# Convolutional feed-forward: seven half-block products for eight in the down projections of the full turns, with the sums kept tokens-on-partitions

## What is computed

```python
def conv_ffn(h, w_up, conv_w, conv_b, w_down):
    seq = h.shape[1]
    u = h @ w_up
    up = jnp.pad(u, ((0, 0), (CONV_W - 1, 0), (0, 0)))
    u = sum(up[:, j:j + seq] * conv_w[j] for j in range(CONV_W)) + conv_b
    a, b = u[..., :D_FF_2], u[..., D_FF_2:]
    return (jax.nn.silu(a) * b) @ w_down

x = x + conv_ffn(rms_norm_2(x, norm_ffn_g[i]), f_w_up[i], f_conv_w[i], f_conv_b[i], f_w_down[i])
```

## Time and profile before

| what | value |
|---|---|
| median of 3 runs | 2540.43 us (2539.84 to 2540.81) |
| the profiled execution | 2541.5 us |
| its span, first to last instruction | 2539.7 us |
| PE busy | 2495.9 us, 98% |
| POOL busy | 1654.6 us, 65% |
| DVE busy | 1280.0 us, 50% |
| ACT busy | 795.7 us, 31% |
| granted TensorE clock | 0.998 of full speed |

### The profile page before, as it was taken

One profiled execution on the slowest core, in us unless ns is written; L12 is line 12 of the kernel. 1 busy time (PEld: TensorE's weight loads), 2 busy tenths in 40 slices (PEclk: granted clock), 3 DMA queues, 4 the chain that ended last, 5 costly groups with the idle time before them and its releaser, 6 DMA issues.

```text
span 2539.7 us, 34091 instructions
## 1 busy us (share of the span) xinstructions
PE 2495.9 (98%) x12467; PEld 2033.0 (80%) x12467; DVE 1280.0 (50%) x2205; ACT 795.7 (31%) x1405; POOL 1654.6 (65%) x2010
## 2 busy tenths in 40 slices
PE   8999999999999999999989999999999999999999
PEld 6778788887787878888667888888888887888887
DVE  7444765427666567533785443435343243543432
ACT  3443432215545434322554211113112113311111
POOL 5355677866664666686652777777665755877774
PEclk9999999999999999999999999999999999999999
DMA  5122555532221366452320333232322321433231
GB/s 145 43 78 83 133 139 143 133 100 79 71 82 51 101 132 151 131 133 75 100 68 25 93 100 100 91 105 87 100 74 76 99 68 65 117 100 100 89 110 67
DMA packets 281536, 243.50 MB, mean 96 GB/s; under 512 B 14291, under 2 KB 247740, under 8 KB 281276
## 3 DMA queue, kind: packets, MB, share of 16 engines
q1 hardware_dynamic: 267692, 216.11, 27.9%
q0 software_dynamic: 13056, 25.17, 5.9%
q10 hardware_dynamic: 656, 0.43, 0.1%
HBM read 239.59 MB, written 2.10 MB: 95 GB/s over the span
## 4 chain that ended last, share of the span: by engine, by line
PE 80%; DVE 11%; issue 3%; POOL 2%; ACT 2%; DVEq 1%; DMA 1%; ACTq 0%; POOLq 0%
PE proj L753 21%; PE proj L755 21%; PE proj L754 21%; POOL w_lo L1916 2%; PE proj L2993 1%; PE proj L2994 1%; PE proj L2992 1%; DVE s_lo L1426 1%; DVE top L2508 1%; DVEq L2511 1%; PE aux L1301 1%; PE aux L1302 1%; PE aux L1303 1%; PE proj L1301 1%; PE aux L3006 1%
## 5 line engine op out<-in xcount | busy, mean ns | idle before, releaser
L753 PE MATMUL proj<-a_hi,w_hi 128*128 128x512 f32 x1864 | 739.2, 397 | 0.1
L755 PE MATMUL proj<-a_hi,w_lo 128*128 128x512 f32 x1864 | 726.5, 390 | 0.0
L754 PE MATMUL proj<-a_lo,w_hi 128*128 128x512 f32 x1864 | 726.0, 389 | 0.0
L1964 POOL TENSOR_TENSOR pool_carrier<-small 128x1 f32<-128x1 f32 x393 | 92.7, 236 | 660.6 <-PE proj L755 545.7
L1987 POOL TENSOR_TENSOR w_lo<-raw,w_hi 128x512 fp32r<-128x512 f32 (+2 forms) x393 | 517.6, 1317 | 5.3
L1986 POOL TENSOR_TENSOR w_lo<-raw,w_hi 128x512 fp32r<-128x512 f32 x330 | 430.6, 1305 | 27.5
L753 PEld LDWEIGHTS proj<-a_hi,w_hi 128*128 128x128 f32 x1864 | 350.2, 188 | 81.3 <-issue 9.1
L755 PEld LDWEIGHTS proj<-a_hi,w_lo 128*128 128x128 f32 x1864 | 350.2, 188 | 74.0
L754 PEld LDWEIGHTS proj<-a_lo,w_hi 128*128 128x128 f32 x1864 | 350.4, 188 | 73.6 <-issue 2.9
L753 PE MATMUL proj<-g_hi,w_hi 128*128 128x512 f32 x720 | 283.5, 394 | 2.5 <-DVE g_lo L740 2.3
L755 PE MATMUL proj<-g_hi,w_lo 128*128 128x512 f32 x720 | 280.4, 389 | 0.0
(11 more groups left out here) (430 smaller groups left out, 3810.7 us busy)
## 6 DMA issues: line engine op xcount, KB each, us to landing
raw<-in_mlp_w SPq DMA_DIRECT2D x52, 1024.0 KB, 5.5
raw<-in_f_w_up SPq DMA_DIRECT2D x88, 512.0 KB, 4.9
raw<-in_b_w_in SPq DMA_DIRECT2D x24, 1024.0 KB, 5.2
F<-in_mlp_w POOLq DMA_DIRECT2D x36, 512.0 KB, 5.7
raw<-in_f_w_down SPq DMA_DIRECT2D x18, 1024.0 KB, 5.2
raw<-in_hgrn_w_in SPq DMA_DIRECT2D x32, 512.0 KB, 4.9
raw<-in_b_w_out SPq DMA_DIRECT2D x8, 1024.0 KB, 5.0
F<-in_mlp_w SPq DMA_DIRECT2D x6, 1024.0 KB, 7.9
```

The costliest lines, as they stand in the source:

```text
L753: pe.matmul(psum[r][:], w_hi[r][:, w], xh, start=k == 0 and not begun, stop=False, skip_group_check=begun)
L754: pe.matmul(psum[r][:], w_hi[r][:, w], xl, start=False, stop=False, skip_group_check=begun)
L755: last = pe.matmul(psum[r][:], w_lo[r][:, w], xh, start=False, stop=k == kc - 1, skip_group_check=begun)
L1964: pool.tensor_tensor(pool_carrier[:], zero, zero, ALU.add)
```

## The change

Both full turns of both layers become seven stages. `ffn_stages` builds two `SevenStage`s of 8 pair slabs and two quarter slabs, and one stage for the last 6 blocks. `SevenStage` takes the number of its up units from its slabs (16 here, 8 in the MLP). The methods for sums, weights and products move from `Mlp` into a common class `Sevens`, and `Ffn` derives from it. `Ffn` keeps its four first products in F, its sums s1 and s4 share a PSUM bank with the silu side, and s2 lies in SBUF (`log_ms`). The products are added into `acc`. In the first layer the last stage turns these sums by 32 transposes into its banks; in the second layer DVE adds the last stage's banks into `acc`, where ACT and DVE copied before. The retention tables share space with the sums and are loaded later. The main part of the diff:

```diff
+            sevens = [seven_stage(pairs(t * DC, DC), down, t) for t in range(FULL)]
...
             def pe(self, pe):
...
+                    for j in range(0 if t else 2, st.ups):
+                        unit(pe, st, j, DC, a_hi, a_lo)
+                    self.seven_pe(pe, st, t)
...
+                pe.wait_ge(*taken_sums(self.sevens[-1], 7))
+                unit_pair(pe, st, 2 * size, size, g_hi, g_lo, 0, self.split.low.at,
+                          lambda u: self.turn_sums(pe, psum[st.bank(u)], u - 2 * size, BOTH))
...
             def act(self, act, h_at):
...
+                    act.activation(u, self.x[s][j % 2], ACT.Identity, bias=conv_col(self.l, 3, c),
+                                   scale=conv_col(self.l, 2, c)).then_inc(tap2.sem, 1)
+                    if st.SEVEN and j >= DC - 2:
+                        self.high_weights(act, st, j - (DC - 2), s)
+                    if s == 0:
+                        act.wait_ge(*tap0.at(2 * j))
+                        act.activation(self.x[0][j % 2], u, ACT.Silu).then_inc(silu.sem, 1)
+                for t, st in enumerate(self.sevens):
+                    for j in range(DC):
+                        first = j < KS
+                        gate(st, self.taps[t], j, 0, t * DC + j)
+                        if 1 <= j <= KS:
+                            self.high_first_sum(act, t, j - 1)
+                        elif j > KS:
+                            self.high_second_sums(act, t, j - 1 - KS)
+                        gate(st, self.taps[t], j, 1, t * DC + j + FF2C)
+                        act.wait_ge(*self.whole.at(j, t))
+                        there, src = (self.LEFT, self.kept[j]) if first else (slice(0, T), self.raw_at[j % 2])
+                        act.copy(tile(g_hi, j)[:, there], src[:, there]).then_inc(self.x_high.sem, 1)
+                    self.high_second_sums(act, t, KS - 1)
+                    for p in range(2, st.PRODUCTS):
+                        for h in range(2):
+                            self.high_weights(act, st, p, h)
...
             def dve(self, dve, then=None):
...
+                    for j in range(DC):
+                        if j >= KS + 2:
+                            dve.wait_ge(*self.low_at("s4", j - 2 - KS, t))
+                        project(st, j, 0)
+                        if 1 <= j <= KS:
+                            self.first_rows(dve, t, j - 1)
+                        elif j > KS:
+                            self.second_rows(dve, t, j - 1 - KS)
+                        if j == DC - 1:
+                            self.low_weights(dve, st, 0)
+                        mix(st, taps, j, 0, t * DC + j)
+                        project(st, j, 1)
+                        if 1 <= j <= KS:
+                            self.first_sum(dve, t, j - 1)
+                        elif j > KS:
+                            self.second_sums(dve, t, j - 1 - KS)
+                        if j == DC - 1:
+                            self.low_weights(dve, st, 1)
+                        mix(st, taps, j, 1, t * DC + j + FF2C)
+                        product(taps, j, self.kept[j] if j < KS else self.raw_at[j % 2]).then_inc(self.whole.sem, 1)
+                    self.second_rows(dve, t, KS - 1)
+                    self.second_sums(dve, t, KS - 1)
+                    self.take_products(dve, st, t)
...
+                if self.l == 1:
+                    for n in range(2):
+                        for b in range(TB):
+                            bank = self.out_arrived(dve, st, size, n, b)
+                            sums = acc[:, bass.ds(b * D + n * T, T)]
+                            dve.tensor_tensor(sums, bank[:], sums, ALU.add).then_inc(dve_out.sem, 1)
+                    return
...
-                        if st is st_dsa_o and q == 0:
+                        if st is ffn[0].st and q == 4:
+                            sp.wait_ge(unit_done, st.before.done(st.before.at(6, 1)))
                             ret_tables()
```

More of the change, by code:

```diff
@@ L415, in program, with seven_stage, quarter @@
         SEVENS = FF // D - 1
+        def seven_stage(ups, down, t):
+            def quarter(k, n):
+                return down[:, t * DC + k * KS:t * DC + (k + 1) * KS, n * T:(n + 1) * T]
+            quarters = [Slab(KS, units, lambda i, n=n: [(0, T, quarter(1, n))], across=True) for n, units in ((0, 14), (1, 0))]
+            stages.append(SevenStage(stages[-1], ups + quarters, sum(st.SEVEN for st in stages), t, quarter))
+            return stages[-1]
         def mlp_stages(l):
@@ L421, in ups @@
                 return [plain(mlp_w1[l], col=lambda i, c=c: t * D + c * 256) for c in range(4)]
[L423 to L430, removed]
+            sevens = [seven_stage(ups(t), down, t) for t in range(SEVENS)]
             return sevens, stage(1, ups(SEVENS) + [plain(mlp_w2[l], k0=SEVENS * DC, col=lambda i, c=c: c * 256) for c in range(4)])
@@ L1639, in down_by_token @@
             def down_by_token(self, pe, st, size, split):
-                before, _, size_before, *_ = self.parts[0]
-                for c in range(DC):
-                    emptied(pe, before, 2 * size_before + c, before.turns - 1)
                 for n in range(2):
@@ new lines, in pe @@
+                for t, st in enumerate(self.sevens):
+                    if t == 0:
+                        unit(pe, st, 0, DC, a_hi, a_lo, ready=self.pre.low.at)
+                        unit(pe, st, 1, DC, a_hi, a_lo)
+                        self.pre.norm.sum(pe)
+                    for j in range(0 if t else 2, st.ups):
+                        unit(pe, st, j, DC, a_hi, a_lo)
+                    self.seven_pe(pe, st, t)
+                st, size = self.st, self.size
+                for j in range(2 * size):
+                    unit(pe, st, j, DC, a_hi, a_lo)
@@ L1726, in dve @@
+                st, first, size, split = self.st, self.first, self.size, self.split
+                for j in range(size):
+                    for s in range(2):
+                        gate(st, self.taps[FULL], j, s, first + j + s * FF2C)
+                    act.wait_ge(*split.whole.at(j))
+                    act.copy(tile(g_hi, j), self.x[1][j % 2]).then_inc(split.high.sem, 1)
             def dve(self, dve, then=None):
                 dve.wait_ge(*self.pre.norm.ready())
-                l = self.l
@@ new lines, in dve, with rest @@
+                st, first, size, split, taps = self.st, self.first, self.size, self.split, self.taps[FULL]
+                dve.wait_ge(*taken_sums(self.sevens[-1], 7))
+                def rest(j):
+                    dve.wait_ge(*split.high.at(j))
+                    dve.tensor_tensor(tile(g_lo, j), self.x[1][j % 2], tile(g_hi, j).bitcast(F32),
+                                      ALU.subtract).then_inc(split.low.sem, 1)
+                for j in range(size):
+                    for s in range(2):
+                        project(st, j, s)
+                        if s == 0 and j >= 1:
+                            rest(j - 1)
+                        mix(st, taps, j, s, first + j + s * FF2C)
+                    product(taps, j, self.x[1][j % 2]).then_inc(split.whole.sem, 1)
@@ L1770, in program @@
+                then.dve_paced(dve, DC - 1)
         ffn = [Ffn(0)]
```

469 lines of the change are left out of this document (230 added, 239 removed).

## The result

| | before | after |
|---|---|---|
| median | 2541.51 us (2539.66 to 2545.21) | 2547.55 us (2544.92 to 2550.72) |
| the profiled execution, its span | 2541.5, 2539.7 us | 2544.92, 2543.1 us |
| ratio, with its 95% interval | | 1.0022 [1.0015, 1.003] |

The change makes the kernel slower by 0.2%: 6 us between the medians, 3.4 us between the two profiled executions (the one of after is the quickest of its runs). The forecast was 2541.6 us with a range of 2536 to 2558: the median is inside the range and 6.0 us above the forecast.

A forecast was written before the change was run, and what follows sets the result against it. PE was taken as the bound: -21.8 us of matmuls, +3.5 transposes, +19.4 waits, +0.1 at the end gave +1.2 us on the base median of 2540.43, so 2541.6 us; range 2536 to 2558.

The forecast's parts named there:

- PE's rate and what bounds the kernel: Whole kernel: PE, 98% busy, is the only limit; 96 fewer matmuls at 0.2267 us each save 21.8 us.
- The chain behind the last up unit: Full feed-forward turns: serial DVE and ACT work on the last block makes product 2 start 2.53 us late.
- E: Time at which PE starts its next work after the last up unit; the chain is laid out from it.
- low weights 1: DVE's low weights for product 1: start at about E + 2.94 and last 1.2 us if run at once.
- the low weights 2: DVE's low weights for product 2, made after product 0's two sums: end at E + 13.36.
- The gaps behind it: PE waits after product 2 starts: 0.99, 0.20 and 0.20 us, with restarts 2.20 us a turn.
- rival B: POOL takes the port before DVE's low weights 1: 8.34 us lost a turn, 2555.6 us; chance 0.32 in all turns.
- The step by which I judged it: Port race: decided by whether ACT's cast of product 1's half 1 ends before DVE reaches low weights 1, or after.
- Transposes: First layer's last stage: 32 transposes turning the sums back to channels, 0.11 us each, 3.5 us in all.
- Edits costed at nothing: Up-phase DVE work, table loads, quarter landings: 0; next turn's first unit 0, up to 1 us; the end +0.1 us.
- The sum of 1.2: Whole kernel, in us: -21.8 matmuls, +3.5 transposes, +19.4 waits in four turns, +0.1 at the end.
- rival B in some turns: Mixed case in which POOL takes the port in only some full turns: 2546 to 2551 us; chance 0.08.

The follow-up runs named there:

- Experiments 3 and 4: Changed kernel: 3 makes low weights 2 before product 0's sums, 2541.84 us; 4 casts half of product 2's weights, makes low weights 2 around last block's sums, 2534.26 us.
- experiment 7: Two kernels against the changed one: one-column operations delay DVE's last remainder, 2560.72 us, or delay it and POOL's transfer, 2562.34 us.
- the second kernel: Changed kernel with five one-column DVE operations before the last remainder in each full turn, and 1 to 4 on POOL before its transfer: 2562.34 us.
- experiment 8: Changed kernel with every turn of the sums in the first layer's last stage issued twice, 32 more transposes: 2555.88 us; also two more profiles of the kernel before.
- experiment 1: The changed kernel once more, unaltered, timed beside the kernel before: 2548.37 us, ratio 1.0024.
- experiment 5: Like the kernel casting half of product 2's weights before the last block's sums, but ACT casts both halves there: 2554.07 us, ratio 1.0044.

## Why the prediction was right, and where it wasn't

**PE's rate and what bounds the kernel.** Right. 96 matmuls of 0.2267 us are gone, and the turn whose only loss is in the forecast's gaps loses 4.84 us against that.

**The chain behind the last up unit.** Right to a tenth of a microsecond. Timeline of DVE in after, in the turn that the earlier trace rows took E from (here E = 1628.98):

```profile
1630.68 1.09 DVE L1389 TENSOR_TENSOR s_lo<-F,s_hi 128x256 fp32r<-128x256 f32 x1
1631.69 0.41 DVE L1392 TENSOR_TENSOR s_lo<-aux,s_hi 128x256 fp32r<-128x256 f32 x1
1632.02 1.21 DVE L1340 TENSOR_TENSOR w_lo<-raw,w_hi 128x1024 fp32r<-128x1024 f32 x1
1633.16 1.52 DVE L1802 SCALAR_TENSOR_TENSOR F<-aux,cols,F 128x511 f32<-128x511 f32 x2
...
1636.13 0.69 DVE L1374 TENSOR_TENSOR g_lo<-aux,g_hi 128x512 fp32r<-128x512 f32 x1 [0.65 <-ACT g_hi L1776]
...
1641.22 1.21 DVE L1340 TENSOR_TENSOR w_lo<-F,w_hi 128x1024 fp32r<-128x1024 f32 x1
```

The low weights 1 start at E + 3.04 (forecast 2.94), the low weights 2 end at E + 13.45 (13.36), and product 2 starts at E + 13.51 (13.41). The remainder with two SBUF inputs was held for POOL as forecast. Experiments 3 and 4 show that this chain and nothing else sets product 2's start.

**The gaps behind it.** Right: 0.99, 0.20, 0.20, released by POOL, DVE and DVE; the 0.99 is missing where the clock fell.

**The port, forecast against rival B.** The outcome was right, in 28 turns of the seven kernels that left this place alone. The step by which I judged it was wrong. I wrote that it decides whether the cast of half 1 ends before DVE reaches the low weights 1. The cast ended 0.10 us before, where I had it 0.02 us behind, and DVE ran all the same. By my own step rival B would have come in every turn; that the forecast came in its place was luck. The point lies 0.16 to 0.21 us behind the end of the cast (experiment 7), so the change missed rival B by about a tenth of a microsecond. Rival B's price was near: 8.34 forecast, 8.8 to 9.6 measured, and 2560 to 2564 us for the kernels that met it in three or four turns, against 2555.6. By the Trainium skill (SBUF — State Buffer, "Who interferes with whom"), whoever issues first holds the pair. The runs agree for a whole POOL pair of remainders, if "issues" is read as the moment at which its last input is signalled and not as a recorded start: the records of POOL's pair begin 0.63 us after DVE's held operation in the fourth turn of the second kernel (2411.69 against 2411.06).

**Transposes.** Mis-sized a little: 3.8 us for 3.5. The transposes themselves and the slow step behind each group take 0.11 (experiment 8: 0.10), and the missing 0.3 us lies in the steps of the matmuls right behind them, up to 0.233 for 0.2267 us.

**Edits costed at nothing.** The up phases show no gap, and 15 units of a second turn take 81.53 us for 81.60. The end costs nothing: from the last scaling to the end of the span 39.25 us before and 39.28 after. The first unit of the next turn was costed at nothing with up to 1 us, and costs 0.72 in one turn of four (and 1.1 in one of four of experiment 1). That was one of the prediction's signs of being wrong, and it came true in this turn. Timelines of ACT and POOL in after show why:

```profile
1665.25 1.05 ACT L1334 CAST w_hi<-F 128x1024 fp32r<-128x1024 f32 x1 [1.55 <-DMA F<-in_f_w_down]
1666.44 2.55 POOL L2011 TENSOR_TENSOR w_lo<-F,w_hi 128x512 fp32r<-128x512 f32 x2 [3.89 <-ACT w_hi L1334]
```

The last added quarter lands late, ACT's cast waits for it, and POOL is free for the next unit only behind that. From its issue to its landing it took 7.3 us in this turn and 6.5 to 6.8 in the three turns without the gap. I had taken the MLP's landings for these, and by the page the median is 6.3 us here and 5.7 there.

**What was not in the sum.** The clock: a fall behind the 2.4 us gap, in two to three turns of four, 0.36 us net. No row of before shows such a gap in this place, and I didn't ask what PE would do behind one. With it and the late unit a first-layer turn loses 5.20 and 5.91 us. By the scalings of DVE all four turns lose another 0.3 us each, 5.1 to 6.1, in steps between matmuls that are each a few thousandths over 0.2267 and that no single row shows. So the four turns lose 21.8 us for 19.4, the transposes take 0.3 more, and the layers' first turns are 0.2 and 0.5 us longer to their 16th unit, since the first scaling, from which I measure, starts earlier against PE. Against that, the four other up phases are 0.07 us shorter each, and the end doesn't cost its 0.1. That makes +4.2 us for the two layers of the first pair of profiles. The stretch between them is 0.4 shorter. The sum of 1.2 was short by 3 us in the layers and by another 2 ahead of them, and the base was 1 us low: 2540.43 us from three runs, 2541.51 from ten. Neither alters which mechanism sets the time.

**The range.** The forecast of a turn was meant to hold within 1 us, which made 2537 to 2546. The median of 2547.55 lies above that, in the band that I had given to rival B in some turns (2546 to 2551). The time alone would have pointed to a mechanism that the trace shows in no turn. It is inside 2536 to 2558 only because the range was widened for rival B, and that much is luck too. One reading of rival B's evidence was also a little off: of the six MLP turns with a held operation, five show 3.8 us and the first 3.98.

## What to carry to other kernels

- When fewer instructions on the critical engine are bought with a longer chain of preparation, lay that chain out in time before counting what is saved. Here 5.44 us of matmuls were paid with 4.84 us and more of waiting, and one reordering of a cast and a subtraction, not one instruction less, gave 14 us back.
- A step that two engines race for should be given a margin. Look for the operation whose input is signalled last on the other engine, and keep it late on purpose: casting both halves early costs 20 us against casting one.
- Filling PE's idle time with matmuls, to hold its clock, brought nothing here, where the weights behind it were the next thing to be late.

## What the runs showed of the hardware

- A DVE operation with both inputs in SBUF that starts 0.16 us after the event that releases POOL's two remainders (the end of ACT's cast) runs in 1.21 us; so do 28 that start some 0.10 us after it. Those that start 0.21 to 0.77 us after it, eleven of eleven, take 4.2 to 4.7 us, until both of POOL's are over. POOL's own record starts later than DVE's, and a transfer issue in between, from 0.15 to 0.64 us ahead of DVE, makes no difference.
- DVE doesn't get in between POOL's two back-to-back remainders: the held operations end about their own length behind the end of the second (1509.02 against 1507.93 for the low weights of 1.2 us, 2281.92 against 2281.63 for a remainder of 0.4).
- Behind idle gaps of 2.4 us PE's granted clock fell to the lower level for 3.4 us in some turns and not in others (two and three of four in two profiles of the same kernel). Behind gaps of 3.8 us it fell in four turns of four (experiment 5). With the gap cut to between 1.2 and 1.3 us or filled, no fall was seen in either feed-forward layer.
